# RWKV recurrence on one core: bonus, gate, heads and rests cut into one part per step, and the output product begun ahead of the last centring

## The reference, cut to what matters

```python
def step(S, inp):
    r_t, w_t, k_t, v_t, a_t, b_t = inp
    sa = jnp.einsum('bhvk,bhk->bhv', S, a_t)
    S = S * w_t[:, :, None, :] + sa[..., None] * b_t[:, :, None, :] + v_t[..., None] * k_t[:, :, None, :]
    y = jnp.einsum('bhvk,bhk->bhv', S, r_t)
    return S, y
...
y = wkv7(rh, wh, kh, vh, -kk, kk * ah)
mean = jnp.mean(y, axis=-1, keepdims=True)
var = jnp.mean(jnp.square(y - mean), axis=-1, keepdims=True)
y = (y - mean) * lax.rsqrt(var + GN_EPS) * gn_g.reshape(H, N).astype(f32) + gn_b.reshape(H, N).astype(f32)
y = y + jnp.sum(rh * kh * r_k.astype(f32), axis=-1, keepdims=True) * vh
out = (y.reshape(B, T, C).astype(h.dtype) * g) @ wo
```

## Time and profile before

| what | value |
|---|---|
| runs (median of three) | 1414.84 us, from 1411.49 to 1429.83 |
| span of the profiled execution, first to last instruction | 1422.4 us |
| PE busy in it | 1372.8 us, 97% |
| DVE, ACT busy | 913.7 us (64%), 706.0 us (50%) |
| the stage of the change in it | about 872 to 965 us |

### The profile page before, as it was taken

The page is one execution under the profiler, slowest core; times in us unless marked ns, Lnnn a source line. Parts: engine busy times, 40 slices in busy tenths (PEclk is TensorE's granted clock), DMA queues, the critical chain, the costliest instruction groups (busy, mean ns, idle before and its releaser), DMA issues. The chain is left out here.

```text
span 1422.4 us, 28871 instructions
## 1 busy us (share of the span) xinstructions
PE 1372.8 (97%) x12692; PEld 1314.1 (92%) x12692; DVE 913.7 (64%) x1419; ACT 706.0 (50%) x1098; POOL 8.2 (1%) x14
## 2 busy tenths in 40 slices
PE   7999999999899999999999899999999996999999
PEld 7999999888799999999998677889999995999999
DVE  4665566557785546666588763667666668666664
ACT  5444455356564446444458333446444466554442
POOL 0000000000000000000000010000000000000000
PEclk9999999999999999999999998999999999999999
DMA  7555555461344344655524021114555541255552
GB/s 272 208 179 191 194 180 179 182 264 60 119 178 178 129 151 156 214 182 197 199 85 176 31 91 60 61 60 167 190 197 207 190 149 60 94 204 178 178 184 84
DMA packets 33109, 222.48 MB, mean 156 GB/s; under 512 B 3879, under 2 KB 5295, under 8 KB 6616
## 3 DMA queue, kind: packets, MB, share of 16 engines
q1 hardware_dynamic: 31928, 219.57, 42.7%
q10 hardware_dynamic: 1056, 1.07, 0.2%
HBM read 219.55 MB, written 1.07 MB: 155 GB/s over the span
## 5 line engine op out<-in xcount | busy, mean ns | idle before, releaser
L315 DVE TENSOR_TENSOR tile_lo<-ring,tile_hi 128x1024 fp32r<-128x1024 f32 x388 | 466.0, 1222 | 276.8 <-ACT tile_hi L305 276.2
L305 ACT ACTIVATE tile_hi<-ring 128x1024 fp32r<-128x1024 f32 x388 | 399.5, 1053 | 250.8 <-PE ps L357 245.8
L355 PE MATMUL ps<-hT_hi,tile_hi 128*128 128x256 f32 x1664 | 467.5, 281 | 5.0 <-DVE tile_lo L315 1.8
L356 PE MATMUL ps<-hT_lo,tile_hi 128*128 128x256 f32 x1664 | 463.4, 278 | 0.0
L357 PE MATMUL ps<-hT_hi,tile_lo 128*128 128x256 f32 x1664 | 463.4, 278 | 0.0
L355 PEld LDWEIGHTS ps<-hT_hi,tile_hi 128*128 128x128 f32 x1664 | 315.0, 189 | 10.6 <-issue 4.6
L356 PEld LDWEIGHTS ps<-hT_lo,tile_hi 128*128 128x128 f32 x1664 | 312.9, 188 | 0.0
L357 PEld LDWEIGHTS ps<-hT_hi,tile_lo 128*128 128x128 f32 x1664 | 312.7, 188 | 0.0
L355 PE MATMUL ps<-hidden_hi,tile_hi 128*128 128x256 f32 x864 | 241.2, 279 | 0.0
L357 PE MATMUL ps<-hidden_hi,tile_lo 128*128 128x256 f32 x864 | 241.2, 279 | 0.0
L356 PE MATMUL ps<-hidden_lo,tile_hi 128*128 128x256 f32 x864 | 241.2, 279 | 0.0
(11 more groups left out here) (467 smaller groups left out, 1997.5 us busy)
## 6 DMA issues: line engine op xcount, KB each, us to landing
ring<-stream SPq DMA_DIRECT2D x204, 1024.0 KB, 4.8
x_sb<-x SPq DMA_DIRECT2D x4, 256.0 KB, 4.0
bias<-f_dram ACTq DMA_DIRECT2D x1, 1024.0 KB, 8.1
fox_bias<-forget_dram SPq DMA_DIRECT2D x1, 1024.0 KB, 6.2
squares<-mem SPq DMA_DIRECT2D x1, 1024.0 KB, 4.7
out<-x_sb SPq DMA_DIRECT2D x4, 256.0 KB, 2.2
const_sb<-const SPq DMA_DIRECT2D x1, 581.0 KB, 9.8
small_sb<-small SPq DMA_DIRECT2D x1, 493.5 KB, 9.5
```

The lines of the kernel that those rows point to most:

```text
L305: act.activation(e.w_hi[:, n % SPLIT, :], e.ring[:, tile % RING, span(n % 2, HALF)], ACT.Copy).then_inc(e.tile_hi.handle, 1)
L315: dve.tensor_tensor(e.w_lo[:, n % SPLIT, :], e.ring[:, CUT[n // 2] % RING, span(n % 2, HALF)], e.w_hi[:, n % SPLIT, :].bitcast(F32), ALU.s ...
L355: pe.matmul(out, left[0], right[0], start=start, stop=False)
L356: pe.matmul(out, left[0], right[1], start=False, stop=False)
```

## The change

Seven edits, all in the steps of the recurrence and at its end.

- `heads_after` and `rests_after` take a limit (`most`, four halves if not given).
- ACT's four heads of the output tiles, which stood ahead of its loop, go one each to the ends of steps 3, 5, 7 and 9.
- DVE's four rests, which stood together in step 9, go one each to steps 10 to 13.
- The bonus product of DVE (128 x 2048 in step 0) becomes two of 128 x 1024, in steps 1 and 2, and the product of gate and gain (128 x 2048 in step 8) becomes four of 128 x 512, in steps 6 to 9.
- The four `turn` of PE go from steps 3 to 6 to steps 4 to 7, and the two products of `given` after each from DVE's steps 4 to 7 to steps 5 to 8.
- The rescaling of `e.x`, in pairs in steps 10 to 13, goes to steps 3, 4, 5 and 9.
- ACT's `heads(0)` and `heads(1)`, which stood behind the last copy of `y` and behind `centre(2)`, go behind the copy of step 17 and ahead of that of step 18; PE's `centre(3)`, which stood ahead of `half_tile(0, 0)`, goes into its middle.

```diff
-def heads_after(e, act, done):
-
-    while may_split(e.hi_issued, done):
+def heads_after(e, act, done, most=4):
+
+    for _ in range(most):
+        if not may_split(e.hi_issued, done):
+            return
...
             def turn(b):
-                pe.wait_ge(*boosted.at(1))
+                pe.wait_ge(*boosted.at(2))
...
-                if 3 <= n < 7:
-                    turn(n - 3)
+                if 4 <= n < 8:
+                    turn(n - 4)
...
-            centre(3)
...
-            half_tile(0, 0)
+            half_tile(0, 0, between=lambda: centre(3))
             sums(1)
...
-            heads_after(e, act, 2 * g0)
             for n in range(1, N + 3):
+                if n == 18:
+                    heads(1)
...
+                if n in (3, 5, 7, 9):
+                    heads_after(e, act, 2 * g0, 1)
                 if n == 13:
                     square_root(0)
-                if n == 18:
+                if n == 17:
                     heads(0)
             centre(2)
-            heads(1)
             centre(3)
...
-                if n == 0:
-                    dve.tensor_tensor(flat(w.ep).rearrange("p (h d) -> p h d", d=HD), heads_of_v(w),
-                                      w.bonus[:, :, :].rearrange("p t h -> p (t h)").unsqueeze(2).to_broadcast([P, TT * RH, HD]),
+                if n in (1, 2):
+                    dve.tensor_tensor(boost[:, n - 1, :].rearrange("p (h d) -> p h d", d=HD),
+                                      w.v[:, n - 1, :].rearrange("p (h d) -> p h d", d=HD),
+                                      w.bonus[:, n - 1, :].unsqueeze(2).to_broadcast([P, RH, HD]),
                                       ALU.mult).then_inc(*boosted.one())
...
-                if n == 8:
-                    dve.wait_ge(*given_ready.at(4))
-                    link.done(dve.tensor_tensor(gate[:, :, :], gate[:, :, :], small(e, "gn_g").unsqueeze(2).to_broadcast(
-                        [P, KC, SEQ]), ALU.mult))
-                if n == 9:
-                    rests_after(e, dve, 2 * g0)
+                if 6 <= n < 10:
+                    b = n - 6
+                    dve.wait_ge(*given_ready.at(b + 1))
+                    link.done(dve.tensor_tensor(gate[:, two(b), :], gate[:, two(b), :],
+                                                small(e, "gn_g")[:, two(b)].unsqueeze(2).to_broadcast([P, 2, SEQ]), ALU.mult))
                 if 10 <= n < 14:
-                    for k in (2 * n - 20, 2 * n - 19):
+                    rests_after(e, dve, 2 * g0, 1)
+                if n in (3, 4, 5, 9):
+                    b = (3, 4, 5, 9).index(n)
+                    for k in (2 * b, 2 * b + 1):
```

More of the change, by code:

```diff
@@ L307, in heads_after, with rests_after @@
         e.hi_issued += 1
-def rests_after(e, dve, done):
-    while may_split(e.lo_issued, done):
+def rests_after(e, dve, done, most=4):
+    for _ in range(most):
+        if not may_split(e.lo_issued, done):
+            return
         n = e.lo_issued
@@ L3097, in _ @@
                                   e.ps[:, b:b + 2, 0:384].bitcast(I32), keep, ALU.bitwise_and).then_inc(*gram_kept.one())
-                if n == 0:
-                    dve.tensor_tensor(flat(w.ep).rearrange("p (h d) -> p h d", d=HD), heads_of_v(w),
-                                      w.bonus[:, :, :].rearrange("p t h -> p (t h)").unsqueeze(2).to_broadcast([P, TT * RH, HD]),
+                if n in (1, 2):
+                    dve.tensor_tensor(boost[:, n - 1, :].rearrange("p (h d) -> p h d", d=HD),
+                                      w.v[:, n - 1, :].rearrange("p (h d) -> p h d", d=HD),
+                                      w.bonus[:, n - 1, :].unsqueeze(2).to_broadcast([P, RH, HD]),
                                       ALU.mult).then_inc(*boosted.one())
-                if 4 <= n < 8:
-                    dve.wait_ge(*turned.at(n - 3))
+                if 5 <= n < 9:
+                    dve.wait_ge(*turned.at(n - 4))
                     for i in range(2):
-                        pair = 2 * (n - 4) + i
+                        pair = 2 * (n - 5) + i
                         x = dve.scalar_tensor_tensor(out=given[:, pair, :], in0=e.ps[:, 7, span(i, SEQ)],
```

## The result

The changed kernel takes 1445.56 us, median of four runs from 1433.92 to 1457.48, beside 1415.32 us for the kernel before. The ratio is 1.0138 with an interval of 1.0088 to 1.0188: slower beyond that interval, though by less than 2%, where 1407.7 us was forecast. The ratio leaves out the slowest run of the changed kernel, 1457.48 us, and stands for some 20 us, while the two medians lie 30 us apart.

A forecast was written before the change was run, and what follows sets the result against it. PE, busy for 97% of the span, was taken as the bound, so only its standstill and low clock could be won: 1.56 + 4.73 + 0.20 + 0.63 = 7.1 us off the 1414.84 us median, 1407.7 us, range 1400 to 1416 us.

The forecast's parts named there:

- four terms: In the recurrence: 1.56 us wait at the start, 4.73 us low clock, 0.20 us in step 11, 0.63 us at the end.
- The second rival: Steps 3 to 13 stretch because moved heads and rests aren't covered by PE: 8.5 us price, 1416.2 us, chance 0.05.
- The range: Forecast time between 1400 and 1416 us, leaving out the second rival and the slow end of run-to-run spread.
- every case lies within 2%: Whole kernel: the verdict stays within 2%, which is 28 us, in every case seen; chance 0.97.
- The start: PE's wait before the second `right_side` of the recurrence goes, 1.56 us, and the clock stays high, 4.73 us.
- the term of 4.73 us: Recurrence up to step 5's gram: cost of the low clock, expected to vanish; bounds 0 and 4.73 us.
- either alone leaves most of the wait: At the start, moving only the heads or only the bonus would leave most of the 1.56 us wait.
- the 1.56 us: PE's wait for DVE before the second `right_side` of the recurrence, expected to go whole; put between 1.0 and 1.56 us.
- The first rival: The clock falls all the same at the recurrence's start or soon after: 2.4 us left, 1412.4 us, chance 0.27.
- The cut products: DVE's smaller products cost 0.48 us more for the gate, less for the bonus, covered by PE's steps.
- Step 11: Recurrence step where `right_side` begins 1.05 instead of 0.85 us after its gram; spreading the rests wins 0.20 us.
- The end: Two PE waits around `centre(3)` ahead of the output product go, 0.38 + 0.25 = 0.63 us; bounds 0 and 0.63.

The follow-up runs named there:

- e2: The kernel before with only the two helpers limited to four halves per call: 1453.02 us, ratio 1.0196 (1.0145 to 1.0248).
- e9: The code of e1 once more, with more runs: 1409.3 us, median of twelve, beside 1419.59 us for the kernel before; ratio 0.9949 (0.9915 to 0.9983).
- e1: The changed kernel with the helpers' default limit raised from 4 to 99: 1419.05 us, median of ten; ratio to the kernel before 0.9986 (0.9947 to 1.0026).
- e3: The kernel before, limited to four halves only at the third feed-forward's last call, ahead of keys and values: 1439.09 us, ratio 1.0103 (1.0043 to 1.0163).
- e6: e1 with DVE's bonus product whole again in step 0: recurrence stretch 71.1 us, against 63.2 us in e1; one run, only stretches compared.
- e5: e1 with ACT's four heads ahead of its loop again: recurrence stretch 64.0 us, against 63.2 us in e1; one run, only stretches compared.
- e7: e2 with the limit at five halves: keys and values 21.3 us as before, end of the window's attention 26.0 us against 19.8 us before; one run.
- e8: e3 with 33 identity products on PE ahead of the wait at keys and values: that stretch 28.9 us, against 36.4 us in e3; one run.
- e10: e1 with gate, rests and rescaling whole and in their old steps: recurrence stretch 64.3 us, against 63.2 us in e1; one run.

## Why the prediction was wrong

**The step that failed** is the one that has no line in it: the new parameter of `heads_after` and `rests_after`. The prediction's sum has four terms, all in the recurrence, and takes "the same 7.1 us off the median", as if every other call issued what it did: everything outside the stage stood at nothing, without a reason. The list of the change made the same mistake, as it put all seven edits in the recurrence. But the helpers are called from all stages, and at four ends of stages a call had issued five or six halves. The limit alone (e2) costs 28 us by its ratio. Without it, e9 shows the forecast's gain (0.9949) and e1 a ratio whose interval holds it. The second rival, steps that stretch, was the only one on the slower side, and it isn't what happened: PE has no new bracket in any step of the recurrence. The range and the sentence that every case lies within 2% rested on the same omission. The ratio of 1.0138 lies within 2% all the same; that of e2, 1.0196, only just does, and its interval reaches to 1.0248.

**The start** was right in mechanism: 6.28 us by the trace for 6.29 us. That the two agree to 0.01 us is in part luck, as both are held against the one execution of the kernel before in which the low clock lasted 10.3 us. It lasted 6.7 us in e2 (883.4 to 890.1), 13.5 us in e3 (877.5 to 891.0) and 13.6 us in e6, so the term of 4.73 us is one of several sizes. That "either alone leaves most of the wait" was right for moving the heads alone, where 1.55 us of the wait stay (e6), and wrong for splitting the bonus alone, where 0.75 us stay (e5). That is near what the rows had, 876.7 - 875.98 = 0.72 us, and with that wait the clock doesn't fall. That the clock hangs on the 1.56 us is shown by e5 and e6 side by side, one execution each, and by five executions with the old start (69.0 to 72.2 us in the kernel before, e2, e3, e7 and e8, the last two 70.7 and 70.5 us) against those with the new one (63.2 us in the changed kernel, e1 and e9). The first rival, a clock that falls all the same, showed in none of them.

**The cut products** cost what the rows had and lay hidden: 0.68 us for a quarter of the gate, 1.22 us for half the bonus. The Trainium skill's formula for an fp32 `tensor_tensor` add (VectorE: DVE Perf Modes, The TRN2 errata — SBUF-src ops pay a fixed extra latency per instruction), taken for these products, gives an estimated 0.69 and 1.22 us for them. The trace agrees. DVE was no bound here.

**Step 11** gave its 0.20 us; but e10 shows that the pieces carry 1.1 us once `turn` has moved, a coupling that the prediction didn't look for. **The end** was mis-sized: 0.92 us for 0.63 us. The prediction had the centring moved and not saved. But the moved one takes 943.52 - 942.85 = 0.67 us between matmuls of the output product, where it stood in 1.13 us of its own between two waits. That would be 0.46 us more than the brackets, of which some 0.3 us show at `sums(1)`; where the rest went is open.

## What to carry to other kernels

A parameter with a default is an edit of every call: ask at each call how many times the loop ran before, and read the order of all stages, counts included, not of the changed one. A late half of a tile at a stage's start costs its wait and what the clock takes behind it: as much again at the keys and values (7.6 and 7.5 us), but only 1 to 2 us behind the waits of 4.50 and 5.63 us at the two other places. So the calls between stages are where weight splitting must run ahead. And a cheap product ahead of a chain's first link can cost more than its length, if the wait that it makes is the one that brings the clock down: the bonus takes 2.28 us and, standing there, cost 7.9 us (e6).

## What the runs showed of the hardware that was not expected

The fp32r matmuls of 256 columns come at one of two distances, some 0.113 or 0.118 us, and keep it through most of a feed-forward stage, with the granted clock at 1.00 in both. In one execution of e9, two windows of 50 us in the first and the last feed-forward hold 441 and 426 of them:

```profile
100.00:150.00 50.00, 50.00 (x441) 50.00 (x441) 30.90 (x32) 21.92 (x24) 0.00 (x0) 1.00 0.57 197
1300.00:1350.00 50.00, 50.00 (x426) 50.00 (x425) 30.95 (x31) 22.85 (x27) 0.00 (x0) 1.00 0.52 187
```

In e1, the same code, it is 427 in the first of these stages and 440 in the last. In all twelve traces each of the four feed-forward stages, past its start and short of its end, settles at one of the two (over a hundred matmuls 0.113 to 0.115 or 0.118 us each). A stage takes about 5 us more or less by it (147.2 or 152.1 us in the third), so by an estimate up to 4 x 5 = 20 us of a run's time can differ between executions of the same code, nearly three times what the recurrence won; the twelve runs of e9 lie between 1405.17 and 1425.84 us. What sets the distance stays open: it follows neither kernel nor stage. Nor does the chip alone set it, as both distances come in one execution. That it changes from run to run of one kernel on one chip isn't shown, since e1 and e9 ran on different chips, and no experiment here was made on it.
